# Second block of a two-block model kernel: banks of the attention gate, order and banks of the index products, bank of the key's rope, pace of attention

## The chip, the cores and the metric

The program runs on one core of a Trainium2 chip. The metric is the device time of one execution in microseconds, from the first to the last instruction with what lies around them. Engines are named as in the profile: PE is TensorE's matmuls, PEld its weight loads, DVE is VectorE, ACT is ScalarE, POOL is GpSimd, SP issues most DMAs.

## What is computed

The reference is a first block (gated delta rule, window attention, a feed-forward layer and a mixture of eight experts) followed by a second block of two layers. Only the second block is touched. Each of its layers does this on 256 rows of width 1024:

```python
h = rmsnorm(x, norm_g[l])
q, k, v, ga, iq, ik, iw, xr, gr, ma, mb = jnp.split(h @ w_in[l], offsets, axis=-1)
q, k = apply_rope(q), apply_rope(k)           # 8 heads of 128
iq, ik = apply_rope(iq), apply_rope(ik)       # 16 index heads of 64, one index key
...
dots = jnp.einsum('bqhd,bsd->bqhs', iqb, ik)
idx_score = jnp.einsum('bqh,bqhs->bqs', iwb, jax.nn.relu(dots))
_, sel = lax.top_k(idx_score, topk)           # 64 of up to 256 keys, per query
... # softmax attention of q over the chosen k, v
y_a = (attn * jax.nn.silu(ga)) @ w_out_attn[l]
hr = rg_lru(causal_depthwise_conv_2(xr, ...)) # gated linear recurrence
y_b = (hr * jax.nn.silu(gr)) @ w_out_rnn[l]
x = x + (sigmoid(ma) * y_a + sigmoid(mb) * y_b) @ w_o[l]
```

## The kernel before

**Weights.** All is float32. A projection is cut into tiles of 128 output columns. ScalarE casts the tile's weights to fp32r (`hi`, L1816), VectorE subtracts to get the low part (`lo`, L2436; "the split"), and TensorE does three fp32r matmuls for each of 8 slices of the depth (`mm3`, L864 to L866): 24 matmuls of 128x256 a tile. Five such weight slots exist in this part, so cast and split of a piece can run up to five tiles ahead. SP loads two tiles' weights with one DMA of 1 MB.

**Order of a layer.** Every engine has its own program in program order, tied by semaphores, and all of them walk through the same list (`fm(...)`, TensorE L1747 to L1772, ScalarE L2385 to L2406, VectorE L3272 to L3290): v, xr, ik and iw, iq, then q, k, ga (8 tiles each), gr (11), ma and mb (8 each), then the output products ya, yb and o. `fm` takes tiles in pairs; a pair fills one of the eight PSUM banks, and the banks in its third argument are used in turn. Before a bank is written, `claim(b)` waits for the step that was noted as its last reader. q and k use banks 0 to 3 and are emptied by ScalarE. ga and gr are emptied by ScalarE's tanh and then by VectorE, which multiplies by the bank once more (`silu`, L3258 to L3263).

**Side work in ticks.** Between tiles `fm` calls `tick()`, which runs one step of a generator. `ticks=2` gives one after each tile; `ticks=3` gives one after the first tile of a pair and two after the second. During q, k and ga the generator is `index_steps` (24 ticks, called I1 to I24 here); during gr and ma it is `attention_steps` (A1 on; gr gives 12 ticks, with A11 and A12 together after its eleventh tile). `also=rn` advances the recurrence (`rnn_steps`) by half a step after every second pair: its matmuls are L1739, on ScalarE it is tanh, exp and square root with table loads (L2364 to L2376), on VectorE four operations ending in a scan (L3244 to L3251), always some tiles behind ScalarE.

**Index.** I1 is the rope product of ik, I2 to I5 those of iq (`rope`, L1676): one matmul with a rotation matrix into bank 4 or 5, read by VectorE's first rope operation (L3154), after which two more follow (L3155, L3158). The bank is `4 + (i // 2) % 2`, so ik's and the first iq's are both in bank 4. From I7 on come the index products (L1701): 12 ticks, each filling one bank, 4 and 5 in turn, with products of 64 rows for two heads of 256 keys (eight ticks) or four heads of 128 keys (four ticks). A tick takes heads of one row half only: even heads lie in rows 0 to 63, odd ones in rows 64 to 127. ScalarE applies relu a bank per tick (L2343, two buffers), VectorE multiplies by iw and adds (L3190). After the last product VectorE picks the 64 greatest by eight rounds of max and match-replace (L3204, L3207).

**Attention.** A1 to A8 are the ropes of q and k in the same two banks, A9 is empty. Then six units of four 128x128 blocks go through `attend` (11 steps, A10 to A20): scores (L1713), mask and maximum on VectorE (L2783 to L2789), exponentials on ScalarE (L2110), reciprocal (L2797), scaling (L2126), transposes (L870, bank 4), their copy (L2118), products with v (L1721, bank 5), the gate (L3227).

Of the kernel before, what the change touches and what calls it, by code (L numbers as in the profile page):

```python
# [14 lines left out]
T = 256  # L15
# [14 lines left out]
C_ID, C_ONE, C_ROTA, C_ROTI, C_TRIL, C_LT, C_IOTA = range(7)  # L30
# [235 lines left out]
def _program(nc, ctx, p, out):  # L266
    S = Signals(nc, ctx)
    up, at = S.up, S.at
# [12 lines left out]
    bank = [ctx.enter_context(nc.psum_tensor(f"bank{i}", [128, 512], F32)) for i in range(8)]  # L281
# [24 lines left out]
    def C(k):  # L306
        return consts[:, k * 128:(k + 1) * 128]
# [546 lines left out]
    def tensor_program(pe):  # L854
# [4 lines left out]
        def claim(b):  # L859
            if b in busy:  # L860
                pe.wait_ge(*at(*busy[b]))
# [810 lines left out]
        for l in range(2):  # L1672
            t_ = T_l[l]
            if l == 0:
                h_cols(0, 0)
            def rope(Xt, n, rotc, name, l=l):  # L1676
                for i in range(0, n, 2):
                    m = min(2, n - i)
                    b = 4 + (i // 2) % 2
                    claim(b)  # L1680
                    pe.matmul(bank[b][:, 0:m * T], rotc, Xt[:, i:i + m, :].rearrange("p a b -> p (a b)"), start=True, stop=True).then_inc(*up("rot", l, name, i))
                    busy[b] = ("rot_sin", l, name, i)
                    yield

            def index_steps(l=l):
                pe.wait_ge(*at("iq", l, 6))
                yield from rope(L2.IK.unsqueeze(1), 1, C(C_ROTI), "ik")
                yield from rope(L2.IQ, 8, C(C_ROTI), "iq")
                yield
                pe.wait_ge(*at("roped", l, "iq", 6))  # L1690
                nr = 0
                for n in (1, 0):
                    wd = 128 * (n + 1)
                    nh = 512 // wd
                    for g in range(0, 16, 2 * nh):
                        for par in range(2):
                            b = 4 + nr % 2
                            claim(b)
                            for i in range(nh):
                                h = g + par + 2 * i  # L1700
                                k = pe.matmul(bank[b][:, i * wd:(i + 1) * wd], L2.IQ[64 * par:64 * par + 64, h // 2, n * 128:n * 128 + 128],  # L1701
                                              L2.IK[64 * par:64 * par + 64, 0:wd], start=True, stop=True)
                            k.then_inc(*up("dots", l, nr))
                            busy[b] = ("relu", l, nr)
                            nr += 1
                            yield
                for r in range(5):
                    yield

            def qk2(u, q, o, l=l):  # L1710
                hs, wd, n = u
                pe.wait_ge(*at("roped", l, "k", 6))
                return pe.matmul(o, L2.QT[:, hs[q], n * 128:n * 128 + 128], L2.KT[:, hs[q], 0:wd], start=True, stop=True)  # L1713

            def pv2(u, i, b, l=l):
                hs, wd, n = u
                nt = wd // 128
                pe.wait_ge(*at("v", l, 1, 1))
                for q in range(4):
                    h, kt = q // nt, q % nt  # L1720
                    k = pe.matmul(bank[b][:, h * 128:(h + 1) * 128], L2.VV[:, kt, hs[h] * 128:(hs[h] + 1) * 128], L2.pT[:, i % 2, q * 128:(q + 1) * 128], start=kt == 0, stop=kt == nt - 1)  # L1721
                return k

            def attention_steps(l=l):
                pe.wait_ge(*at("k", l, 6))
                yield from rope(L2.QT, 8, C(C_ROTA), "q")
                yield from rope(L2.KT, 8, C(C_ROTA), "k")
                yield
                yield from attend(DSA_UNITS, l, ((2, 3), (4,), (5,)), qk2, pv2, 2)

            def rnn_steps(l=l):

                for n in range(8):
                    h = 2 * (n % 2)
                    pe.wait_ge(*at("rnn_xc", l, n))
                    for q in range(2):
                        claim(6 + q)
                        for j in range(2):
                            k = pe.matmul(bank[6 + q][0:88, j * T:(j + 1) * T], L2.WR[:, q, h + j, :], L2.XC[:, h + j, :], start=True, stop=True)  # L1739
                    k.then_inc(*up("rnn_mm", l, n))  # L1740
                    busy[6], busy[7] = ("rnn_exp", l, n), ("rnn_ix", l, n)
                    yield
                    yield

            rn, ix, at_ = rnn_steps(), index_steps(), attention_steps()
            rm_first(t_["v0"][0], XT, (0, 1), (("h", l),), ("v", l, 0), lambda l=l: h_cols(l, 1))
            lane.back[:] = [rn]  # L1747
            fm(t_["xr"], XT, (2, 3, 0, 1), ("xr", l))
            rm(t_["v1"], XT, (0, 1), ("v", l), c0=1)
            tick()  # L1750
            x = t_["ik"]
            _, w = piece_view(W, x)
            pe.wait_ge(*at("lo", x))
            claim(4)
            for k in range(8):
                k_ = mm3(bank[4][:, 0:T], sl(w, ALL, k), sl(XT, ALL, k), k == 0, k == 7)
            k_.then_inc(*up("used", x))
            narrow(bank[4][:, T:T + 64], t_["iw"], 16, 4)
            busy[4] = ("iw", l)
            fm(t_["iq"], XT, (2, 3, 0, 1), ("iq", l), pace=lambda nb: nb % 2)  # L1760
            lane.back[:] = [ix]
            fm(t_["q"], XT, (0, 1, 2, 3), ("q", l), ticks=2, also=rn)
            fm(t_["k"], XT, (0, 1, 2, 3), ("k", l), ticks=2, also=rn)
            fm(t_["ga"], XT, (0, 1), ("ga", l), ticks=2, also=rn)
            lane.finish(ix)
            lane.back[:] = [at_]
            fm(t_["gr"], XT, (0, 1), ("gr", l), ticks=2, also=rn)
            fm(t_["ma"], XT, (0, 1), ("ma", l), ticks=3, also=rn)
            lane.finish(at_)
            lane.back[:] = [rn]  # L1770
            fm(t_["mb"], XT, (0, 1, 2, 3), ("mb", l), pace=lambda nb: 1)
            lane.finish(rn)  # L1772
            pe.wait_ge(*at("o_cols", l, 5))
            fm_raw(t_["ya"], L2.GA, (0, 1, 2, 3), ("ya", l), 8)
            pe.wait_ge(*at("hr_gated", l))
            fm_raw(t_["yb"], L2.GR, (0, 1, 2, 3), ("yb", l), 11)

            def o_ready(k, l=l):
                if k % 2 == 0:
                    pe.wait_ge(*at("lo_merge", l, k))  # L1780
            out_proj(XT, t_["o"], (4, 5, 6, 7), o_ready, (lambda: h_cols(1, 0)) if l == 0 else None)
            for t in range(2):
                for h in range(2):
                    busy[4 + 2 * t + h] = ("resid", l, t, h)
# [19 lines left out]
    def scalar_program(a):  # L1804
# [508 lines left out]
        for l in range(2):  # L2313
# [81 lines left out]
            lane.back[:] = [ix]  # L2395
            fm(t_["q"], to(L2.QT, "q"), ticks=2, also=rn)
            fm(t_["k"], to(L2.KT, "k"), ticks=2, also=rn)
            fm(t_["ga"], tanh_to(L2.GA, "ga_th", 2), ticks=2, also=rn)
            lane.finish(ix)
            lane.back[:] = [at_]  # L2400
            fm(t_["gr"], tanh_to(L2.GR, "gr_th", 2, [(f"xr_out{i}", l) for i in range(3)]), ticks=2, also=rn)
            fm(t_["ma"], tanh_to(L2.MA, "ma", 2), ticks=3, also=rn)
            lane.finish(at_)
            lane.back[:] = [rn]
            fm(t_["mb"], tanh_to(L2.MB, "mb", 4), pace=lambda nb: 1)
# [22 lines left out]
    def vector_program(v):  # L2428
# [714 lines left out]
        for l in range(2):  # L3143
            t_ = T_l[l]

            def rope(Xt, n, cos, sin, name, l=l, state=[None, None]):
                for i in range(0, n, 2):
                    m, s = min(2, n - i), (i // 2) % 2
                    x2 = Xt[:, i:i + m, :]
                    r_ = L2.rt[:, s, 0:m * T].rearrange("p (a b) -> p a b", a=m)  # L3150
                    v.wait_ge(*at("rot", l, name, i))
# [12 lines left out]

            def index_steps(l=l):
                v.wait_ge(*at("cos", 1))
                yield from rope(L2.IK.unsqueeze(1), 1, cosI, sinI, "ik")
                yield from rope(L2.IQ, 8, cosI, sinI, "iq")
                yield
                yield  # L3170
# [84 lines left out]
                    run(n)  # L3255
                    yield

            def silu(dst, name, l=l):  # L3258

                def f(i, m, nb, x):  # L3260
                    d = dst[:, i:i + m, :]
                    v.wait_ge(*at(name + "_th", l, i))
                    v.scalar_tensor_tensor(d, d, 1.0, bank[nb % 2][:, 0:m * T].rearrange("p (a b) -> p a b", a=m), ALU.add, ALU.mult).then_inc(*up(name, l, i))  # L3263
                return f

            def gated(l=l):
# [12 lines left out]
            lane.back[:] = [ix]  # L3279
            fm(t_["q"], None, ticks=2, also=rn)  # L3280
            fm(t_["k"], None, ticks=2, also=rn)
            fm(t_["ga"], silu(L2.GA, "ga"), ticks=2, also=rn)
            lane.finish(ix)
            lane.back[:] = [at_]
            fm(t_["gr"], silu(L2.GR, "gr"), ticks=2, also=rn)
            fm(t_["ma"], None, ticks=3, also=rn)
            lane.finish(at_)
            lane.back[:] = [rn]
            fm(t_["mb"], None, pace=lambda nb: 1)
# [137 lines left out]
```

## Time and profile before

| | us |
|---|---|
| median of 3 runs | 2372.04 |
| lowest, highest | 2367.88, 2376.61 |
| the profiled execution | 2379.05 |
| its span | 2377.2 |
| TensorE, VectorE, ScalarE busy | 2261.4, 1695.3, 1421.5 |

The second block's first layer begins at about 1550 us of the span, the second at about 1966 us. The profile gives the busy time of each engine, the granted clock of TensorE, groups of instructions by line, who waited for whom, and the instructions in order of time. A bracket behind an instruction, such as [2.87 <-DVE work L3154], is the idle time of its engine just before it and what ended that. Matmuls are pipelined: one may be shown to start before the last has ended. A float32 matmul that is not fp32r shows as two records.

### The profile page before, as it was taken

How to read it: one execution, taken by the hardware profiler on the slowest of the kernel's cores; microseconds unless marked ns; L12 is line 12 of the kernel's file. 1: busy time of each engine (PE TensorE's matmuls, PEld its weight loads, DVE VectorE, ACT ScalarE, POOL GpSimd, SP SyncE). 2: the span in 40 equal slices, each digit the busy share in tenths (PEclk: the TensorE clock that was granted, in tenths of full speed). 3: DMA queues.
4: the chain of work that ended last, by engine and by line, in shares of the span. 5: the costliest groups of instructions: out<-in, count | busy, mean ns of one | idle time of the engine just before them, and what ended most of it. 6: DMA issues, size and time to landing. Idle time of an engine off the chain costs nothing.

```text
span 2377.2 us, 34395 instructions
## 1 busy us (share of the span) xinstructions
PE 2261.4 (95%) x13903; PEld 1984.1 (83%) x13903; DVE 1695.3 (71%) x2152; ACT 1421.5 (60%) x1894; POOL 316.0 (13%) x314
## 2 busy tenths in 40 slices
PE   7889999989999999999999999979998999999898
PEld 7778999877878888888888888769887988888897
DVE  5634655778899999999899999754687335469624
ACT  5432444556787878787777778645556324555722
POOL 0510000000000000000000000006445002553400
PEclk9899999998999999999999999989999999999999
DMA  9421655528899999999999999837444465644343
GB/s 249 126 80 64 233 193 173 173 72 292 315 371 376 363 350 367 356 361 349 363 355 356 357 354 367 305 103 226 131 124 133 125 220 162 193 140 129 114 134 109
DMA packets 328397, 556.42 MB, mean 234 GB/s; under 512 B 23616, under 2 KB 164680, under 8 KB 328232
## 3 DMA queue, kind: packets, MB, share of 16 engines
q1 hardware_dynamic: 318432, 527.63, 63.7%
q0 software_dynamic: 9120, 25.97, 4.6%
q8 instruction: 113, 1.85, 0.3%
q10 hardware_dynamic: 680, 0.54, 0.1%
q14 instruction: 52, 0.43, 0.1%
HBM read 544.12 MB, written 9.96 MB: 233 GB/s over the span
## 4 chain that ended last, share of the span: by engine, by line
PE 82%; DVE 12%; ACT 4%; issue 2%; DMA 0%; SPq 0%; ACTq 0%; DVEq 0%
PE bank L864 22%; PE bank L866 22%; PE bank L865 22%; PE bank L905 6%; DVE parts L2436 3%; PE bank L870 1%; ACT parts L1816 1%; PE bank L1533 1%; PE bank L1701 1%; PE bank L1739 1%; DVE fast L2436 1%; PE bank L1019 1%; PE bank L1594 1%; DVE work L3154 1%; DVE work L3155 1%
## 5 line engine op out<-in xcount | busy, mean ns | idle before, releaser
L2436 DVE TENSOR_TENSOR parts<-raw,parts 128x1024 fp32r<-128x1024 f32 x665 | 809.2, 1231 | 400.7 <-ACT parts L1816 377.3
L1816 ACT CAST parts<-raw 128x1024 fp32r<-128x1024 f32 x665 | 692.0, 1047 | 504.3 <-PE bank L866 490.6
L864 PE MATMUL bank<-cols,parts 128*128 128x256 f32 x1680 | 501.0, 298 | 14.8 <-DVE parts L2436 5.7
L866 PE MATMUL bank<-cols,parts 128*128 128x256 f32 x1680 | 481.9, 287 | 1.1 <-issue 1.1
L865 PE MATMUL bank<-cols,parts 128*128 128x256 f32 x1680 | 482.2, 287 | 0.0
L2436 DVE TENSOR_TENSOR fast<-raw,fast 128x1024 fp32r<-128x1024 f32 x302 | 362.1, 1219 | 32.1 <-ACT fast L1816 14.9
L1816 ACT CAST fast<-raw 128x1024 fp32r<-128x1024 f32 x302 | 315.7, 1052 | 94.1 <-PE bank L866 87.3
L864 PEld LDWEIGHTS bank<-cols,parts 128*128 128x128 f32 x1680 | 330.1, 196 | 32.6 <-issue 19.8
L865 PEld LDWEIGHTS bank<-cols,parts 128*128 128x128 f32 x1680 | 330.1, 196 | 6.2 <-issue 5.4
L866 PEld LDWEIGHTS bank<-cols,parts 128*128 128x128 f32 x1680 | 329.2, 196 | 0.0
L864 PE MATMUL bank<-parts,cols 128*128 128x512 f32 x740 | 294.2, 398 | 13.6 <-DVE parts L2436 6.9
L866 PE MATMUL bank<-parts,cols 128*128 128x512 f32 x740 | 290.6, 393 | 0.0
L865 PE MATMUL bank<-parts,cols 128*128 128x512 f32 x740 | 290.4, 392 | 0.0
L864 PEld LDWEIGHTS bank<-parts,cols 128*128 128x128 f32 x740 | 140.1, 189 | 44.7 <-DVE parts L2436 7.8
L866 PEld LDWEIGHTS bank<-parts,cols 128*128 128x128 f32 x740 | 140.3, 190 | 29.8
L865 PEld LDWEIGHTS bank<-parts,cols 128*128 128x128 f32 x740 | 140.3, 190 | 28.1
L864 PE MATMUL bank<-fast,cols 128*128 128x512 f32 x380 | 149.0, 392 | 0.8 <-DVE fast L2436 0.8
L866 PE MATMUL bank<-fast,cols 128*128 128x512 f32 x380 | 147.9, 389 | 0.0
L865 PE MATMUL bank<-fast,cols 128*128 128x512 f32 x380 | 147.9, 389 | 0.0
L797 POOL DMA_DIRECT2D scr_xr<-work x6 | 4.9, 809 | 1027.0 <-ACT work L2319 1027.0
L905 PE MATMUL bank<-work,raw 128*128 128x256 f32 x608 | 132.1, 378 | 0.0
L905 PEld LDWEIGHTS bank<-work,raw 128*128 128x128 f32 x608 | 114.8, 189 | 16.7
(376 smaller groups left out, 3278.1 us busy)
## 6 DMA issues: line engine op xcount, KB each, us to landing
raw<-in_moe_w_gate_dram SPq DMA_DIRECT2D x112, 1024.0 KB, 6.1
raw<-in_moe_w_up_dram SPq DMA_DIRECT2D x112, 1024.0 KB, 5.9
raw<-in_moe_w_down_dram SPq DMA_DIRECT2D x112, 1024.0 KB, 6.1
raw<-in_w_in_dram SPq DMA_DIRECT2D x76, 1024.0 KB, 5.5
raw<-in_a_w_in_dram SPq DMA_DIRECT2D x12, 1024.0 KB, 11.7
raw<-in_ffn_w_gate_dram SPq DMA_DIRECT2D x11, 1024.0 KB, 5.2
raw<-in_ffn_w_up_dram SPq DMA_DIRECT2D x11, 1024.0 KB, 5.2
raw<-in_ffn_w_down_dram SPq DMA_DIRECT2D x11, 1024.0 KB, 5.0
```

What stands on the lines that cost most here:

```text
L864: pe.matmul(o, l[0], r[0], start=start, stop=False)
L865: pe.matmul(o, l[0], r[1], start=False, stop=False)
L866: return pe.matmul(o, l[1], r[0], start=False, stop=stop)
L870: return pe.transpose(o, i, ident[0:n, 0:n])
L905: k_ = pe.matmul(bank[b][:, j * T:(j + 1) * T], w[:, k, q * 128:(q + 1) * 128], xt[:, k, :], start=k == 0, stop=k == kt - 1)
L1019: k = pe.matmul(o[rs, 64 * j:64 * j + 64], l[rs, j, :], r[rs, j, :], start=True, stop=True)
L1533: k = pe.matmul(bank[b][:, j * 128:(j + 1) * 128], X[:, t, kk * 128:(kk + 1) * 128], N4.P_[:, a, t, :], start=t == 0, stop=t == 1)
L1594: k = pe.matmul(bank[b][:, :], N4.PT[:, e % 2, t, :], N4.y[:, q, 512 * h:512 * h + 512], start=q == 0, stop=q == 1)
L1701: k = pe.matmul(bank[b][:, i * wd:(i + 1) * wd], L2.IQ[64 * par:64 * par + 64, h // 2, n * 128:n * 128 + 128], L2.IK[64 * par:64 * par + 6 ...
L1739: k = pe.matmul(bank[6 + q][0:88, j * T:(j + 1) * T], L2.WR[:, q, h + j, :], L2.XC[:, h + j, :], start=True, stop=True)
L1816: a.copy(dst[0], src).then_inc(*up(o + "hi", x))
L2436: v.tensor_tensor(dst[1], src, dst[0].bitcast(F32), ALU.subtract).then_inc(*up(o + "lo", x))
```

## The change

Four edits, all in the second block and the same in both layers:

- ik's rope product and its VectorE buffer use the other of the two banks (5 instead of 4), with the index `odd=1`.
- An index tick claims banks 4 and 5 together and issues the products of both row halves in alternation, an even head into bank 4 and then an odd one into bank 5; the next tick issues none. ScalarE and VectorE keep a bank per tick.
- ga uses banks 0 to 3 in place of 0 and 1, on all three engines.
- ma's `ticks` is 2 in place of 3.

TensorE's part, then ScalarE's and VectorE's lines:

```diff
-            def rope(Xt, n, rotc, name, l=l):
+            def rope(Xt, n, rotc, name, odd=0, l=l):
                 for i in range(0, n, 2):
                     m = min(2, n - i)
-                    b = 4 + (i // 2) % 2
+                    b = 4 + (i // 2 + odd) % 2
                     claim(b)
...
-                yield from rope(L2.IK.unsqueeze(1), 1, C(C_ROTI), "ik")
+                yield from rope(L2.IK.unsqueeze(1), 1, C(C_ROTI), "ik", 1)
...
                     for g in range(0, 16, 2 * nh):
-                        for par in range(2):
-                            b = 4 + nr % 2
-                            claim(b)
-                            for i in range(nh):
-                                h = g + par + 2 * i
-                                k = pe.matmul(bank[b][:, i * wd:(i + 1) * wd], L2.IQ[64 * par:64 * par + 64, h // 2, n * 128:n * 128 + 128],
-                                              L2.IK[64 * par:64 * par + 64, 0:wd], start=True, stop=True)
-                            k.then_inc(*up("dots", l, nr))
-                            busy[b] = ("relu", l, nr)
-                            nr += 1
-                            yield
+
+                        claim(4)
+                        claim(5)
+                        for i in range(nh):
+                            for par in range(2):
+                                rs, h = slice(64 * par, 64 * par + 64), g + par + 2 * i
+                                k = pe.matmul(bank[4 + par][:, i * wd:(i + 1) * wd], L2.IQ[rs, h // 2, n * 128:n * 128 + 128], L2.IK[rs, 0:wd], start=True, stop=True)
+                                if i == nh - 1:
+                                    k.then_inc(*up("dots", l, nr + par))
+                                    busy[4 + par] = ("relu", l, nr + par)
+                        nr += 2
+                        yield
+                        yield
...
-            fm(t_["ga"], XT, (0, 1), ("ga", l), ticks=2, also=rn)
+            fm(t_["ga"], XT, (0, 1, 2, 3), ("ga", l), ticks=2, also=rn)
...
-            fm(t_["ma"], XT, (0, 1), ("ma", l), ticks=3, also=rn)
+            fm(t_["ma"], XT, (0, 1), ("ma", l), ticks=2, also=rn)
...
-            fm(t_["ga"], tanh_to(L2.GA, "ga_th", 2), ticks=2, also=rn)
+            fm(t_["ga"], tanh_to(L2.GA, "ga_th", 4), ticks=2, also=rn)
...
-            fm(t_["ma"], tanh_to(L2.MA, "ma", 2), ticks=3, also=rn)
+            fm(t_["ma"], tanh_to(L2.MA, "ma", 2), ticks=2, also=rn)
...
-                    m, s = min(2, n - i), (i // 2) % 2
+                    m, s = min(2, n - i), (i // 2 + odd) % 2
...
-            fm(t_["ga"], silu(L2.GA, "ga"), ticks=2, also=rn)
+            fm(t_["ga"], silu(L2.GA, "ga", 4), ticks=2, also=rn)
...
-            fm(t_["ma"], None, ticks=3, also=rn)
+            fm(t_["ma"], None, ticks=2, also=rn)
```

## Rows read from the trace of the kernel before

**Rows 1.** The page, busy time of the engines over the span:
```profile
PE 2261.4 (95%) x13903; PEld 1984.1 (83%) x13903; DVE 1695.3 (71%) x2152; ACT 1421.5 (60%) x1894; POOL 316.0 (13%) x314
```

**Rows 2.** Windows: stretch, length, busy PE, PEld, DVE, ACT, POOL, clock, DMA, GB/s:
```profile
1670.25:1673.40 3.15, 3.15 (x9) 2.12 (x9) 2.88 (x5) 0.00 (x0) 0.05 (x1) 0.50 0.85 246
1690.00:1740.00 50.00, 49.61 (x342) 43.75 (x343) 28.13 (x39) 33.20 (x50) 29.43 (x27) 1.00 0.46 142
1740.00:1757.70 17.70, 17.70 (x148) 17.58 (x147) 16.98 (x42) 9.01 (x11) 0.74 (x1) 1.00 0.31 91
...
1762.36:1765.70 3.34, 3.34 (x16) 3.34 (x17) 3.24 (x13) 2.57 (x4) 3.16 (x4) 0.50 0.04 15
1765.70:1790.00 24.30, 24.12 (x166) 20.52 (x165) 23.85 (x45) 9.16 (x10) 6.12 (x7) 1.00 0.46 143
...
1822.50:1825.50 3.00, 2.94 (x16) 2.80 (x17) 2.66 (x5) 2.38 (x8) 2.82 (x4) 0.72 0.46 161
```

**Rows 3.** Waits of TensorE, 1655 to 1880: total us, times, longest:
```profile
PE bank L870 <- ACT work L2118: 5.8, 2, 4.1
PE bank L1681 <- DVE work L3154: 4.3, 2, 2.9
PE bank L864 <- DVE work L3263: 2.7, 1, 2.7
PE bank L1721 <- issue: 0.9, 1, 0.9
PE bank L1713 <- DVE work L3158: 0.8, 1, 0.8
PE bank L1701 <- DVE work L3158: 0.5, 1, 0.5
```

**Rows 4.** Timeline of TensorE: start, length, line; rope products I2 to I4, gr:
```profile
1670.25 1.22 PE L1681 MATMUL bank<-work 128*128 128x512 f32 x1 [2.87 <-DVE work L3154]
...
1675.67 1.02 PE L1681 MATMUL bank<-work 128*128 128x512 f32 x2
...
1679.39 1.02 PE L1681 MATMUL bank<-work 128*128 128x512 f32 x2
...
1762.36 0.52 PE L864 MATMUL bank<-cols,parts 128*128 128x256 f32 x1 [2.74 <-DVE work L3263]
```

**Rows 5.** Timeline of TensorE, two of the index products' ticks:
```profile
1700.34 1.13 PE L1701 MATMUL bank<-work 64*128 64x256 f32 x4
...
1704.46 1.13 PE L1701 MATMUL bank<-work 64*128 64x256 f32 x4
```

**Rows 6.** Timeline of TensorE, first block: window scores, row halves in alternation:
```profile
475.52 1.23 PE L1463 MATMUL bank<-work 64*128 64x256 f32 x8
```

**Rows 7.** Timeline of VectorE: splits, iq's rope, recurrence, q's first rope:
```profile
1668.63 1.23 DVE L2436 TENSOR_TENSOR parts<-raw,parts 128x1024 fp32r<-128x1024 f32 x1 [6.54 <-ACT parts L1816]
...
1672.36 0.69 DVE L3154 TENSOR_TENSOR work<-bank,work 128x512 f32<-128x512 f32 x1 [0.24 <-PE bank L1681]
...
1683.74 0.68 DVE L3244 SCALAR_TENSOR_TENSOR work<-bank,work 88x512 f32<-88x512 f32 x1
...
1686.97 1.20 DVE L2436 TENSOR_TENSOR parts<-raw,parts 128x1024 fp32r<-128x1024 f32 x1
...
1738.98 1.23 DVE L2436 TENSOR_TENSOR parts<-raw,parts 128x1024 fp32r<-128x1024 f32 x1 [4.83 <-ACT parts L1816]
...
1774.10 0.68 DVE L3154 TENSOR_TENSOR work<-bank,work 128x512 f32<-128x512 f32 x1
```

**Rows 8.** Timeline of ScalarE: relu, transposes' copy, recurrence's first and last operation:
```profile
1714.25 0.60 ACT L2343 ACTIVATE work<-bank 128x512 f32<-128x512 f32 x1
...
1821.85 0.57 ACT L2118 COPY work<-bank 128x512 f32<-128x512 f32 x1
...
1839.88 1.52 ACT L2364 ACTIVATE bank<-bank,work 88x256 f32<-88x256 f32 x4 [2.04 <-PE bank L1739]
...
1844.56 0.63 ACT L2376 ACTIVATE work<-work 88x512 f32<-88x512 f32 x1
```

More of the change, by code:

```diff
@@ L3144, in vector_program, with rope @@
             t_ = T_l[l]
-            def rope(Xt, n, cos, sin, name, l=l, state=[None, None]):
+            def rope(Xt, n, cos, sin, name, odd=0, l=l, state=[None, None]):
                 for i in range(0, n, 2):
-                    m, s = min(2, n - i), (i // 2) % 2
+                    m, s = min(2, n - i), (i // 2 + odd) % 2
                     x2 = Xt[:, i:i + m, :]
@@ L3166, in index_steps @@
                 v.wait_ge(*at("cos", 1))
-                yield from rope(L2.IK.unsqueeze(1), 1, cosI, sinI, "ik")
+                yield from rope(L2.IK.unsqueeze(1), 1, cosI, sinI, "ik", 1)
                 yield from rope(L2.IQ, 8, cosI, sinI, "iq")
@@ L3256, in rnn_steps, with silu @@
                     yield
-            def silu(dst, name, l=l):
+            def silu(dst, name, banks, l=l):
                 def f(i, m, nb, x):
@@ L3262, in f @@
                     v.wait_ge(*at(name + "_th", l, i))
-                    v.scalar_tensor_tensor(d, d, 1.0, bank[nb % 2][:, 0:m * T].rearrange("p (a b) -> p a b", a=m), ALU.add, ALU.mult).then_inc(*up(name, l, i))
+                    v.scalar_tensor_tensor(d, d, 1.0, bank[nb % banks][:, 0:m * T].rearrange("p (a b) -> p a b", a=m), ALU.add, ALU.mult).then_inc(*up(name, l, i))
                 return f
@@ L3281, in vector_program @@
             fm(t_["k"], None, ticks=2, also=rn)
-            fm(t_["ga"], silu(L2.GA, "ga"), ticks=2, also=rn)
+            fm(t_["ga"], silu(L2.GA, "ga", 4), ticks=2, also=rn)
             lane.finish(ix)
             lane.back[:] = [at_]
-            fm(t_["gr"], silu(L2.GR, "gr"), ticks=2, also=rn)
-            fm(t_["ma"], None, ticks=3, also=rn)
+            fm(t_["gr"], silu(L2.GR, "gr", 2), ticks=2, also=rn)
+            fm(t_["ma"], None, ticks=2, also=rn)
             lane.finish(at_)
```

## Prediction

> **What bounds the kernel now.** I read the page first: TensorE (PE) is busy 2261.4 of 2377.2 us, so what is left is small waits, and matmul time that an edit removes [rows 1]. The edits lie in the second block only, in a part that runs once in each of its two layers, 1663 to 1879 us in the first one. Next came TensorE's waits there: six kinds, 15.0 us in all, and in the second layer the same list with the same figures [rows 3]. So I work out one layer and double it. The two long waits that end at 1670.25 and 1762.36 us are each followed by some 3 us at a granted clock of 0.50, that is 1.2 GHz in place of 2.4; the 4.1 us wait is followed by 3 us at 0.72 [rows 2]. A wait thus costs more than itself: from the rope product at 1670.25 to the next is 5.42 us, from that to the one after 3.72 [rows 4], so the low clock cost 1.7 us.
>
> Then the windows by stage. From 1690 to 1740 us (index products) VectorE is busy 28.1 of 50 us, and TensorE is the bound. From 1740 to 1790 us and beyond VectorE is full: 16.98 of 17.70, 23.85 of 24.30 us [rows 2]. It has its last real idle stretch, 4.83 us, at 1738.98 [rows 7], and from there to the last attention scores every TensorE wait is a wait for something VectorE makes. **This second stretch, over 80 us, is as long as VectorE's work in it.** What TensorE saves before it counts only as far as VectorE's stretch starts earlier; what it saves inside counts nothing. Behind it TensorE is the bound again, through the last gate and the output products. Ticks are numbered I1 to I24 for the index (q, k, ga tiles) and A1 on for attention (gr, ma tiles). A tile of 24 matmuls takes 2.87 us: 148 matmuls fill 17.70 us [rows 2].
>
> **Key's rope in bank 5.** Now the first iq rope (I2) claims the bank of ik's rope and waits 2.87 us until VectorE has read it; VectorE itself was held by the weight split at 1668.63 [rows 4, 7]. In its own bank this wait goes, with its 1.7 us of low clock, and the first index product would lose its 0.5 us wait: 5.1 us. But four ropes and one recurrence step must pass VectorE before I7. VectorE was idle for 0.24 us before its first iq rope at 1672.36, so it is free for it at 1672.1; then come four ropes of three operations, some 1.95 us each (0.69 us an operation), three splits of 1.14 and the recurrence, 1683.74 to 1686.97, 3.2 us [rows 7]: 7.8+3.4+3.2 = 14.4, ending at 1686.5. TensorE reaches I7 now at 1679.39 (I4) + 3.72 + 0.85 + 2x2.87 = 1689.7 [rows 4], and 4.57 us earlier at 1685.1. A new wait of 1.4 us stands at I7; I take the clock to hold, since the waits that it fell after are of 2.7 us or more [rows 2, 3]. Gain: 5.1 - 1.4 = **3.7 us**. Bounds: 5.1, and 0 if ScalarE's earlier casts were late as well.
>
> **Index products in pairs.** Twelve ticks carry one bank of products each. The period is 4.12 us [rows 5], less 2.87: 1.25 us a bank. No row shows index products of alternating row halves. The nearest are the first block's window scores, whose 64-row products are issued in just that order into two banks: eight records take 1.23 us, against 1.13 for four of one half [rows 5, 6]. I take that 0.10 more: 1.35 for a pair in place of 2.50. The bounds are no saving (halves one after another) and half, 1.25. The Trainium skill, page "TensorEngine Tiling (Array Packing)", section "Key Properties", says that changing the tiling mode drains TensorE; entering the half-array mode six times and not twelve would by that rule save edges too, and the sum has it in the one 1.25 taken per pair. The same page, section "PSUM Bottleneck", speaks against the change: tiling speeds TensorE up but not the emptying of PSUM. Here ScalarE empties the banks, busy 33.2 of 50 us, and that would still fit in 45 [rows 2].
>
> The new wait: a pair claims both banks, so it needs the relu of the second half, which ScalarE does one tick later, behind a cast and at times a copy. Behind this claim on TensorE stand all its tiles. A relu now ends at 1714.85, 2.15 us after its tile (1704.46 + 2x4.12) [rows 5, 8]; the next pair comes 2.87 after: 0.7 us to spare. After I8 ScalarE also has a recurrence step, 5.3 us and a table load of 1.28 [rows 8]; I follow it through: cast, relu, cast, copy, relu end 12.2 us after I8's tile, TensorE claims at 11.6. One wait of 0.6. To I16 nine singles (11.25) become five pairs (6.75): 4.5 - 0.6 = **3.9 us**. The saving after I16, 2.4 us, falls into VectorE's stretch. VectorE resumes at 1738.98 after a ScalarE cast that hangs on I16's tile [rows 7]; so its stretch starts 3.7 + 3.9 = **7.6 us** earlier, its order and work unchanged.
>
> **Four banks for the attention gate.** Now gr's first tile waits 2.7 us for VectorE's SiLU of the third ga pair [rows 3]. With four banks this wait goes. What is late next: the third q rope (A3) claims bank 4, which VectorE frees at 1774.78, when the first operation of its first q rope ends [rows 7]. TensorE would be there at 1762.36 - 2.74 (wait) - 10.0 (gain up to I18) + 3 tiles (8.6) + 2 ropes (1.7) = 1760, the release comes at 1774.78 - 7.6 = 1767.2. So one wait of 7 us takes the place of 2.7 and two small ones, and 1.7 us of low clock follow, as before. VectorE is not held up (it has the next two ropes' products ahead), so I cost the edit at **nothing**; its cover is VectorE's own queue, and if that should run dry the low clock costs 1.7 a layer.
>
> **Attention over all of the gate ma.** Three ticks per pair of tiles become two, 20 steps in 20 ticks. No DMA is moved, and SP's and POOL's queues keep their order; VectorE and ScalarE do the same steps, each one tile later. Steps A14, A15 now stand back to back, and A15's transposes wait 4.1 us for ScalarE's copy of the first ones, ending 1822.42 [rows 3, 8]. With a tile between, 2.9 of the 4.1 are used. A17, A18 (1.7 us wait) and the last products (0.9) get tiles between too [rows 3]: 2.6. The idle shortened at A15 spares about 0.8 us of clock at 0.72 [rows 2]. Against that, the recurrence step of ScalarE (5.3 us, [rows 8]) now falls after A16, ahead of the copy that A18 needs. Followed through: the step cannot start before A16's casts, scaling, copy and exponentials end, 4.3 us after A16; plus 5.2, cast 0.9, scaling 0.8, copy 0.6 is 11.8; TensorE is at A18 after 9.8 (1.25+1.55+2.9+1.25+2.9). A new wait of 2.0. No later one: A19 comes 4.1 after A18, when ScalarE has just finished. Net: 2.9+2.6+0.8-2.0 = 4.3; around each wait that goes the trace also has edges of 0.1 to 0.2 us (the list of waits leaves them out), some 0.7 in all by my estimate. I take **5.0 us**. Bounds: 2.9 (all else handed back) and 7.
>
> **Sum.** 7.6 + 0 + 5.0 = 12.6 us a layer, 25.2 in two. The profiled execution took 2379.05 us, 7.0 above the median of the runs, and gives 2353.9; against the median, 2372.0 - 25.2 = **2346.8 us**.
>
> **Rivals.** (a) The halves do not overlap, or only as far as VectorE cannot use it: 3.7 + 5.0 = 8.7 a layer, 2354.6 us. For: index operands lie differently from the window's. Against: [rows 6]. (b) VectorE's stretch is not rigid: waits inside it shrink as casts come earlier, the new A18 wait stays out; 16 a layer, 2340 us. The outer bound, all waits (15), low clock (3.8) and pair savings (6.9), is 26 a layer, 2320. (c) VectorE starts no earlier, because ScalarE, not TensorE, sets its cast at 1738.98: then only the attention part is left, 10 us in two layers, 2362 us; the change hardly does what it says. (d) **Slower**: the claim of both banks. If the second relu comes a whole tile late, each of five pair claims waits 2.9 us and 1.7 of low clock follow, 23 us a layer, against gains of 6.9+3.7+5.0 = 15.6: 7.4 lost a layer, 2387 us. It decides the sign when ScalarE lags its tile by 4.3 us rather than 2.15 at each pair (a wait of 1.4 and 1.7 of clock, 3.1 each). For it: one claim is already short. Against: ScalarE is busy only two thirds here [rows 2]. The Trainium skill, page "TensorE: Matmul & The Clock Gate", section on the HAM clock gate, states that an idle TensorE falls back to 1.2 GHz; the 0.50 after 2.87 us agrees [rows 2, 3]. A3's wait of 7 us is where it would strike anew.
>
> **From cases to numbers.** Forecast 0.50, (a) 0.15, (b) 0.14, (c) 0.14, (d) 0.07. The range reaches to (a) and (b) with their bounds, 2337 to 2360, and leaves (c) and (d) out. A measurement of this kernel tells about 0.5% (12 us) from no change: faster 0.79 (forecast, a, b), same 0.14 (c), slower 0.07 (d).
>
> **What would show it.** Right: no wait at I2, a short one at I7; twelve half-array bursts per layer become six of 1.2 to 1.3 us; gr's first tile without a wait and a wait of about 7 us ahead of A3, followed by clock 0.50; VectorE idle last some 7.6 us earlier, counted from the layer's ik rope; about 1 us ahead of A15, 2 at A18. Wrong: bursts of 2.2 us (a), VectorE's stretch shortened (b) or unmoved (c), a wait for relu at every pair (d). All is off if weights come late: the faster tiles need casts and chunks sooner.

## Result and profile after

The changed kernel takes 2348.07 us in the median of 4 runs (2340.6 to 2350.82), the kernel before 2371.29 (4 runs). The ratio is 0.9895, 95% interval 0.9866 to 0.9925; in a later comparison of the same two kernels it was 0.9877 (0.9862 to 0.9892, 2344.16 us in the median of 5 runs). The profiled execution took 2350.82 us with a span of 2349.0, 28.2 us less than the profiled one before. Its engines, from the page; VectorE's and ScalarE's work is the same, TensorE's busy time is 24 us less [rows 1]:

```profile
PE 2237.4 (95%) x13903; PEld 1967.3 (84%) x13903; DVE 1695.4 (72%) x2152; ACT 1420.0 (60%) x1894; POOL 318.9 (14%) x314
```

**Length of a layer.** To compare kernels I take the time from the ik rope product (I1) to the first product with ya's raw weights (L905), since the start of the second block varies from run to run (the ik rope comes at 1664.88 us in one run of the changed kernel and at 1656.60 in another) and hides what a layer gains. Before, TensorE's timeline:

```profile
1663.92 0.60 PE L1681 MATMUL bank<-work 128*128 128x256 f32 x2
...
1879.30 0.81 PE L905 MATMUL bank<-work,raw 128*128 128x256 f32 x3
```

and after:

```profile
1664.88 0.60 PE L1681 MATMUL bank<-work 128*128 128x256 f32 x2
...
1866.57 0.60 PE L905 MATMUL bank<-work,raw 128*128 128x256 f32 x2
```

So 215.38 us before (216.09 in the second layer) and 201.69 after (202.21; 201.66 and 201.70 in the later run): 13.7 us less in the first layer, 13.9 in the second. The two together are the 28.2 us between the profiled executions to within 1 us. The medians are only 23.2 us apart, which is within the scatter of single executions (10 us for the changed kernel). Line numbers behind L1700 are one or two higher than before.

**Waits of TensorE** in the first layer, 1655 to 1870 us, as in [rows 3]:

```profile
PE bank L1681 <- DVE work L3156: 7.2, 1, 7.2
PE bank L870 <- ACT work L2120: 2.2, 2, 1.2
PE bank L1702 <- DVE work L3160: 1.6, 1, 1.6
PE bank L1702 <- ACT work L2345: 1.0, 1, 1.0
PE bank L1715 <- DVE work L3160: 0.8, 1, 0.8
```

12.8 us in place of 15.0 [rows 3]: waits explain 2.2 us of the 13.7. The rest is matmul time: six bursts of products in place of twelve (some 7.5 us) and one stretch of low clock in place of three (some 3 us by my estimate, from the stretches below); about 1 us is left to small gaps. The timeline shows where the new waits are, at I7, I11, A3, A15 and A18, and between them a burst of products that no wait precedes (1711.55) and the rope product that follows A3's (1773.71). Some rows hold fewer records than the burst has, because the stretch that was read ends inside it:

```profile
1687.70 0.49 PE L1702 MATMUL bank<-work 64*128 64x256 f32 x2 [1.58 <-DVE work L3160]
...
1704.55 0.70 PE L1702 MATMUL bank<-work 64*128 64x256 f32 x4 [1.02 <-ACT work L2345]
...
1711.55 1.13 PE L1702 MATMUL bank<-work 64*128 64x256 f32 x8
...
1768.12 1.22 PE L1681 MATMUL bank<-work 128*128 128x512 f32 x1 [7.21 <-DVE work L3156]
...
1773.71 0.59 PE L1681 MATMUL bank<-work 128*128 128x512 f32 x1
...
1815.83 0.63 PE L870 MATMUL bank<-work 128*128 128x128 f32 x4 [1.24 <-ACT work L2120]
...
1832.49 0.52 PE L870 MATMUL bank<-work 128*128 128x128 f32 x3 [0.93 <-ACT work L2120]
```

**Windows** of the same layer (columns as in [rows 2]): index products; VectorE's full stretch up to A3; the 3.3 us after the long wait; from there to the attention scores (A10); the 3 us after A15:

```profile
1688.00:1740.00 52.00, 50.98 (x416) 47.65 (x413) 33.56 (x51) 37.46 (x55) 29.37 (x27) 1.00 0.49 152
1733.00:1768.10 35.10, 27.90 (x217) 26.28 (x215) 34.05 (x91) 21.10 (x28) 14.52 (x15) 0.96 0.40 122
1768.12:1771.40 3.28, 3.28 (x9) 2.25 (x10) 3.25 (x5) 0.00 (x0) 0.00 (x0) 0.50 0.89 272
1771.40:1798.00 26.60, 25.88 (x181) 22.69 (x179) 26.29 (x36) 13.13 (x20) 14.19 (x11) 0.99 0.49 148
...
1815.83:1818.80 2.97, 2.97 (x23) 2.86 (x24) 2.55 (x5) 2.97 (x8) 2.80 (x3) 1.00 0.35 122
```

After the wait of 7.21 us the clock is at 0.50 for 3.28 us, and the low clock costs 1.9 us; after the one of 2.87 us it was 3.15 us and 1.7 us [rows 2, 4]. So here the one long wait costs about as much low clock as one short one did. After A15 the clock is 1.00 in place of 0.72. That 0.72 is a mean over a stretch that begins before the clock falls; in the kernel before, TensorE was at 0.50 here as well, only from some 1.3 us behind the end of the wait:

```profile
1824.00:1827.00 3.00, 3.00 (x16) 3.00 (x15) 2.26 (x5) 2.37 (x7) 2.92 (x3) 0.50 0.01 3
```

VectorE's last idle stretch before it is full ends 67.59 us after the ik rope, and not at 75.06 as before [rows 7], so its stretch starts 7.5 us earlier:

```profile
1732.47 1.22 DVE L2438 TENSOR_TENSOR parts<-raw,parts 128x1024 fp32r<-128x1024 f32 x1 [4.66 <-ACT parts L1818]
```

From there to the first attention scores (A10) it does the same work in the same time, 65.72 us before (first row, from the old trace) and 65.53 after:

```profile
1738.98:1804.70 65.72, 60.62 (x427) 54.22 (x426) 64.20 (x130) 35.00 (x49) 28.66 (x26) 0.97 0.45 136
...
1732.47:1798.00 65.53, 57.60 (x409) 51.76 (x407) 64.14 (x130) 34.76 (x49) 28.71 (x26) 0.95 0.46 141
```

### The profile page after: what moved, and what is told of

The parts are those of the page before. It is cut to its first block, busy times and chain, and to the rows that moved or that the text cites. A ratio compares the mean times of both kernels' runs of the same rounds, so it can differ in the third digit from the quotient of the medians.

```text
span 2349.0 us, 34405 instructions
## 1 busy us (share of the span) xinstructions
PE 2237.4 (95%) x13903; PEld 1967.3 (84%) x13903; DVE 1695.4 (72%) x2152; ACT 1420.0 (60%) x1894; POOL 318.9 (14%) x314
## 4 chain that ended last, share of the span: by engine, by line
PE 79%; DVE 12%; ACT 6%; issue 2%; POOL 1%; DMA 0%; SPq 0%; ACTq 0%; DVEq 0%; POOLq 0%
PE bank L864 22%; PE bank L866 21%; PE bank L865 21%; PE bank L905 6%; DVE parts L2438 3%; ACT parts L1818 2%; PE bank L870 1%; PE bank L1533 1%; PE bank L1019 1%; DVE fast L2438 1%; ACT work L2375 1%; PE bank L1594 1%; POOL work L728 1%; DVE work L3209 1%; ACT bank L2366 1%
## 5 line engine op out<-in xcount | busy, mean ns | idle before, releaser
L905 PE MATMUL bank<-work,raw 128*128 128x256 f32 x608 | 132.1, 378 | 0.0
L905 PEld LDWEIGHTS bank<-work,raw 128*128 128x128 f32 x608 | 114.8, 189 | 16.7
```

Source lines behind the costliest of these rows:

```text
L905: k_ = pe.matmul(bank[b][:, j * T:(j + 1) * T], w[:, k, q * 128:(q + 1) * 128], xt[:, k, :], start=k == 0, stop=k == kt - 1)
```

## Experiments

Theory: up to some point VectorE's work sets the time, and what TensorE saves ahead of it counts only as far as that stretch starts earlier. Rival: each edit is worth the TensorE time that it removes. The first four kernels each undo one edit of the change; "layer" is the length defined above, first and second layer. Where no number of runs is given, the kernel was run once. Since the executions of one kernel scatter over some 10 us, such a run is read by its layers, which for the changed kernel were 201.69 and 202.21 in one run and 201.66 and 201.70 in another: differences of 0.5 us are within the scatter.

**Key's rope back in bank 4.**

```diff
-                yield from rope(L2.IK.unsqueeze(1), 1, C(C_ROTI), "ik", 1)
+                yield from rope(L2.IK.unsqueeze(1), 1, C(C_ROTI), "ik")
```

(and VectorE's line likewise)

> The change with one edit undone: the key's rope is in bank 4 again. Measured length: from the ik rope product to the first product with the raw weights (ya), per layer; 215.4 us before, 201.7 us with the change. Theory (the stretch in which VectorE is full starts later by what TensorE loses ahead of it): the 2.9 us wait at I2 and 1.7 us of low clock are back, the 1.6 us wait at I7 mostly goes, so the layer is longer by 3.7 us: 205.4, the whole kernel by 7.4. Rival (each edit is worth the TensorE time that it removes by itself): 2.9 + 1.7 + 0.5, 206.8. Rival 2 (the gain is swallowed ahead of VectorE's stretch): 201.7.

Measured: 2356.17 us, layer 205.36 and 206.38. The first layer is the theory's 205.4 and not the rival's 206.8. In the second VectorE's full stretch begins 1.3 us later than in the first (72.3 and 71.0 us after the ik rope); why is not shown. The wait of 2.86 us at I2 is back, that at I7 is 0.5 again.

**Index products in twelve ticks again** (TensorE's loop as in the kernel before).

> The change with the index products undone: twelve ticks of one bank again. Theory (VectorE's stretch): what twelve bursts of 1.25 us cost more than six of 1.26 counts up to tick I16 only, less the 1.0 us wait at I11: 4 x 1.25 - 0.05 - 1.0 = 3.9, layer 205.6, and TensorE's wait ahead of A3 shrinks from 7.2 us by the 2.4 us that TensorE loses after I16. Rival (TensorE's own time counts everywhere): 6 x 1.25 - 1.0 = 6.4, layer 208.1, wait ahead of A3 unchanged.

Measured: 2353.8 us, layer 205.70 and 205.93: the theory's 205.6, 2.4 us below the rival. TensorE's waits show that the part of the saving behind I16 had only been waited away again; its wait ahead of A3 is 4.9 in place of 7.2:

```profile
PE bank L1681 <- DVE work L3155: 4.9, 1, 4.9
PE bank L870 <- ACT work L2119: 2.1, 2, 1.2
PE bank L1702 <- DVE work L3159: 1.6, 1, 1.6
PE bank L1714 <- DVE work L3159: 0.8, 1, 0.8
```

**Attention gate back on two banks.**

```diff
-            fm(t_["ga"], XT, (0, 1, 2, 3), ("ga", l), ticks=2, also=rn)
+            fm(t_["ga"], XT, (0, 1), ("ga", l), ticks=2, also=rn)
```

(and the bank counts on ScalarE and VectorE)

> The change with the attention gate back on two banks. Theory (VectorE's stretch): nothing, layer 201.7 within 0.5 us: a wait of some 5 us for the SiLU stands at gr's first tile and the one ahead of A3 shrinks to 1 us or less; VectorE's first q rope starts as long after the ik rope as with the change (102.5 us). Rival (the four banks bring what the removed wait and its low clock cost): longer by 2.7 + 1.5 = 4 us, 206.

Measured: 2350.07 us, layer 201.60 and 201.59. The four banks bring nothing. TensorE now waits 5.0 us for the SiLU at gr's first tile and 1.0 at A7 for a rope, in place of 7.2 ahead of A3, and VectorE's first q rope starts at the same time, 102.4 us after the ik rope (102.5 with the change):

```profile
PE bank L864 <- DVE work L3265: 5.0, 1, 5.0
PE bank L870 <- ACT work L2120: 2.2, 2, 1.2
PE bank L1702 <- DVE work L3160: 1.6, 1, 1.6
PE bank L1702 <- ACT work L2345: 1.0, 1, 1.0
PE bank L1681 <- DVE work L3156: 1.0, 1, 1.0
PE bank L1715 <- DVE work L3160: 0.8, 1, 0.8
```

**Three ticks per pair for ma again.**

```diff
-            fm(t_["ma"], XT, (0, 1), ("ma", l), ticks=2, also=rn)
+            fm(t_["ma"], XT, (0, 1), ("ma", l), ticks=3, also=rn)
```

> The change with three ticks per pair for the gate ma again. Nothing ahead of A14 moves. Waits of 4.1 us at A15, 1.7 at A18 and 0.9 at the end return, those of 1.2 and 0.9 go, the low clock after A15 returns. Theory: the layer is longer by 6.0 us, what the stretch from A15 to ya shortened by: 207.7. Rival (the gain behind A15 came from the earlier start of ScalarE's and VectorE's steps, not from the spacing): 203 or less.

Measured: 2357.6 us, layer 207.80 and 207.97: 6.1 us longer in the first layer, all behind A14. The waits of 4.11, 1.66 and 0.90 us are back. Together the four edits undone one by one cost 3.7 + 4.0 - 0.1 + 6.1 = 13.7 us in the first layer, which is the whole gain of that layer: there they don't interact. In the second layer they cost 4.2, 3.7, -0.6 and 5.8 us, 13.0 before rounding, of 13.9; the scatter of the layers can explain that gap.

**Both banks claimed, but one half after the other.**

```diff
-                        for i in range(nh):
-                            for par in range(2):
+                        for par in range(2):
+                            for i in range(nh):
```

> The change with both banks claimed at once as in it, but the products of the even heads all issued before those of the odd heads. Theory (matmuls of different row halves overlap only when they alternate): a burst takes 2.2 to 2.4 us in place of 1.13 to 1.16, VectorE's full stretch starts 5 x 1.1 less the wait at I11, some 4.5 us later, layer 206. Rival (a burst is short because the matmuls of one tick pay one change of array mode): 1.2 us and 201.7.

Measured: 2344.39 us, layer 202.39 and 202.17, which neither expected. The bursts of eight records are as short as with alternation; those of sixteen are longer, 1.71 us against 1.16. TensorE's timeline of this kernel:

```profile
1705.98 1.14 PE L1702 MATMUL bank<-work 64*128 64x256 f32 x8
...
1713.00 1.71 PE L1702 MATMUL bank<-work 64*128 64x128 f32 x16
```

and of the changed kernel:

```profile
1718.57 1.16 PE L1702 MATMUL bank<-work 64*128 64x128 f32 x16
```

So the halves do overlap, since 1.14 us is what four records of one half take alone [rows 5], but alternation is not needed for it when a half has four records. With eight it matters: the burst is 0.55 us longer, though still shorter than two bursts of one half. One such burst lies ahead of I16, and the product at A3 comes 0.5 us later after the ik rope (103.75 in place of 103.24 us); the layers themselves, 0.7 us longer and not longer at all, are too close to the scatter to show it. What in the array or its queue allows the overlap, these runs don't tell.

**More TensorE work in VectorE's stretch.** The product of A1 is issued four times more, into the same bank with the same operands:

```diff
+                    for _ in range(4 if (name, i) == ("q", 0) else 0):
+                        pe.matmul(bank[b][:, 0:m * T], rotc, Xt[:, i:i + m, :].rearrange("p a b -> p (a b)"), start=True, stop=True)
```

> The change with the first q rope product (A1) issued five times over, the same matmul into the same bank: 4 x 0.85 = 3.4 us more of TensorE work inside the stretch in which VectorE is full. Theory: the wait ahead of A3 shrinks from 7.2 to 3.8 us and the layer stays at 201.7. Rival (TensorE is the bound throughout): 205.1.

Measured: 2345.47 us, layer 202.18 and 201.66. The 3.4 us vanish in the wait, which is 3.76 us now:

```profile
PE bank L1683 <- DVE work L3158: 3.8, 1, 3.8
...
```

**More VectorE work behind A3.** The first operation of the first k rope is done three times more:

```diff
+                    for _ in range(3 if (name, i) == ("k", 0) else 0):
+                        v.tensor_tensor(r_, bank[4 + s][:, 0:m * T]..., sin..., ALU.mult).then_inc(*up("dve"))
+                        v.wait_ge(*at("dve"))
```

> The change with the first operation of the first k rope (A5) done four times over on VectorE: 3 x 0.65 = 1.9 us more of VectorE work inside its full stretch. Theory: the layer is longer by 1.9 us, 203.6, and the wait ahead of A3, which lies before, keeps 7.2. Rival (VectorE has slack there, TensorE is the bound): 201.7.

Measured: 2348.76 us, layer 204.27 and 204.57, 2.6 and 2.4 us longer for the 2.1 us that the three operations take. VectorE has no slack there; whether TensorE has, this run doesn't ask. The three waits for it under one heading, 9.7 us in all, are the old 7.2 and two new ones, 1.9 and 0.6:

```profile
PE bank L1681 <- DVE work L3159: 9.7, 3, 7.2
...
```

**Less VectorE work behind A3.** q's ropes move to the index ticks in which TensorE has no products; for that k's tiles use banks 0 and 1 only and the ropes banks 2 and 3. TensorE's part:

```diff
+                early = rope(L2.QT, 8, C(C_ROTA), "q", 0, 2)
...
                         nr += 2
                         yield
+                        if nr == 4:
+                            pe.wait_ge(*at("q", l, 6))
+                        if nr >= 4:
+                            next(early, None)
                         yield
...
-                yield from rope(L2.QT, 8, C(C_ROTA), "q")
+                for _ in range(4):
+                    yield
```

> The change with q's four ropes taken out of VectorE's full stretch: they run in the product-free ticks I10, I12, I14 and I16 (banks 2 and 3; k's tiles use banks 0 and 1), and A1 to A4 are empty. VectorE is idle for 17.7 us between I7 and I18 with the change. Theory: VectorE's stretch loses 4 x 1.95 = 7.8 us of work, of which up to 2 may come back where ropes delay the weighting and so the relus ahead of I11 to I16; layer 194 to 196, kernel some 12 to 15 us faster than with the change. Rival (another engine, ScalarE with its casts or the A15 chain, is next within 2 us): layer 200 or more.

Measured: 2345.12 us (4 runs), 0.9883 of the kernel before (0.9866 to 0.9899), layer 202.34 and 201.24: nothing over the change. Here the theory fell, and only the rival's number stood. 7.8 us of VectorE work are gone from behind A3, and the waits say what came in their place:

```profile
PE bank L864 <- DVE work L3275: 4.8, 1, 4.8
PE bank L870 <- ACT work L2126: 2.3, 2, 1.3
PE bank L864 <- DVE parts L2444: 2.1, 1, 2.1
PE bank L1703 <- DVE work L3166: 1.6, 1, 1.6
...
```

TensorE waits at gr's fourth tile for a split and at its fifth for gr's first SiLU on bank 0. Both stand in VectorE's queue among or behind the rounds that pick the 64 greatest. From there to A15 it has no wait at all, and now it is TensorE that is full, VectorE no longer:

```profile
1771.40:1811.00 39.60, 38.90 (x275) 35.29 (x274) 35.12 (x50) 24.57 (x53) 22.22 (x20) 0.96 0.52 156
```

In VectorE's timeline of the changed kernel the last operation of the top-k (L3219) ends at 1766.3 us, one split follows, and then the first rope operation, whose end lets TensorE go at 1768.12:

```profile
1766.03 0.30 DVE L3219 TENSOR_SCALAR work<-work 128x256 f32<-128x256 f32 x1
1766.24 1.22 DVE L2438 TENSOR_TENSOR parts<-raw,parts 128x1024 fp32r<-128x1024 f32 x1
1767.38 0.68 DVE L3156 TENSOR_TENSOR work<-bank,work 128x512 f32<-128x512 f32 x1
```

So the wait ahead of A3 is one for **the end of the top-k**, and behind it TensorE, let go late and at half clock, is about as full as VectorE (25.88 and 26.29 of 26.60 us with the change, in the windows above). Slowing VectorE there costs time, and relieving it alone brings nothing. That slowing TensorE there would cost as well is likely but was not tried: the extra work at A1 lay ahead of the wait.

**The same, and gr on four banks**, so that no gr tile needs a SiLU from behind the top-k:

```diff
-            fm(t_["gr"], XT, (0, 1), ("gr", l), ticks=2, also=rn)
+            fm(t_["gr"], XT, (0, 1, 2, 3), ("gr", l), ticks=2, also=rn)
```

> The version with q's ropes early, and gr's tiles on banks 0 to 3 in place of 0 and 1. In the version without this edit TensorE had no wait ahead of A3 any more but one of 2.1 us for a split and one of 4.8 us for gr's first SiLU on bank 0, each followed by low clock, and none from there to A15: layer 202.3 and 201.2 us. Theory (the wait ahead of A3 is a wait for the end of VectorE's top-k, and after it TensorE is the bound as much as VectorE): the 4.8 us and its 1.7 us of low clock go, VectorE's last k rope, which ends some 7 us ahead of A10 + 6.5, is next at A10 with a wait of 4 to 5 us; layer 199 to 200. Rival (VectorE's total work to the attention scores sets the end, whatever the bank): 201 to 202.

Measured: 2332.25 us in its one run, layer 197.53 and 197.57, 4.1 us below the change. The wait of 4.8 us and its low clock went; 1.8 to 2.3 us at A7 and 0.8 at A10, both for k's ropes, came back. That is below the theory's 199 to 200, and not the rival's. One reason is in the trace of the run before: behind its wait of 4.8 us the clock stayed at 0.50 for 5.3 us, 1768.15 to 1773.40, where the theory priced a low clock of 1.7 us. The change with gr on four banks alone, without the early ropes, was not run; since the changed kernel has no wait at any gr tile, I expect nothing of it, but that is argued and not shown.

**k's ropes in A1 to A4 on top of it.**

```diff
-                for _ in range(4):
-                    yield
                 yield from rope(L2.KT, 8, C(C_ROTA), "k")
-                yield
+                for _ in range(5):
+                    yield
```

> As the one before, with k's four ropes in A1 to A4 and the empty ticks in A5 to A8. Theory: the wait at A10 goes too, because the last k rope is done some four ticks earlier; of waits only some 2 us for a split before the end of the top-k, one at A15 and one at A18 stay; layer 195 to 197, kernel 10 to 14 us faster than with the change. Rival (splits behind the ropes become late, TensorE waits for weights in gr): 200 or more.

Measured: 2348.47 us (5 runs), 0.9895 (0.9881 to 0.9908), layer 202.39 and 202.28: the whole gain is lost. I had overlooked that A3's rope then claims bank 4 again before VectorE, still in its top-k, has read A1's. The timeline of TensorE has a wait of 8.29 us there:

```profile
1772.21 2.08 PE L1681 MATMUL bank<-work 128*128 128x512 f32 x2 [8.29 <-DVE work L3161]
```

VectorE's top-k ends at 1770.4 us in this run. As an experiment it confirms what the wait is for: any rope product at A3 that follows one at A1 is held until the top-k ends, q's or k's.

**The changed kernel again, and the best version timed.** Each of these two was compared with the kernel before on its own chip, so they are compared with each other by their ratios.

> The changed kernel once more, beside the other versions and the kernel before on the same chip. Every theory: 0.99 of the kernel before, layer 201.7 to 202.2.

Measured: 2344.16 us (5 runs), ratio 0.9877 (0.9862 to 0.9892), layer 201.66 and 201.70.

> The version with q's ropes early and gr on four banks, timed. Its single run took 2332.25 us and its layers 197.5 us, 4.15 less than with the change. From the layers: 2 x (215.7 - 197.5) = 36.4 us under the kernel before, ratio 0.985 (0.983 to 0.987). If the single run's 41 us stood, 0.983; if the shorter layers were lost elsewhere, 0.988 as with the change.

Measured: 2337.72 us (5 runs, 2332.01 to 2338.51), ratio 0.9841 (0.9827 to 0.9854), layer 197.54 twice. It beats both kernels: 1.6% under the kernel before, and its interval does not meet that of the change. Its waits in the first layer:

```profile
PE bank L864 <- DVE parts L2444: 2.9, 2, 2.1
PE bank L1681 <- DVE work L3162: 2.3, 1, 2.3
PE bank L870 <- ACT work L2126: 2.2, 2, 1.2
PE bank L1703 <- DVE work L3166: 1.6, 1, 1.6
PE bank L1720 <- DVE work L3166: 0.8, 1, 0.8
PE bank L1703 <- ACT work L2351: 0.2, 1, 0.2
```

## The prediction, step by step

Forecast 2346.8 us, measured 2348.07; forecast 12.6 us a layer, measured 13.7 and 13.9. That the total is met within 1.3 us is partly luck: the layers gained 2.4 us more than forecast in all, while the median of the first comparison shows 4.4 us less than the layers do. The later comparison, 2344.16 us, fits the layers better.

**Key's rope, 3.7 us: right.** I7 comes 3.65 us earlier after the ik rope than before, the new wait there is 1.58 us where 1.4 was forecast, and undoing the edit costs 3.7.

**Index products, 3.9 us up to I16: right in sum, with two terms off that cancel.** A pair costs no more than a single bank: 1.13 us for eight records, as long as four took [rows 5], where the window scores let me add 0.10 [rows 6]. The wait at I11 is 1.0 and not 0.6. Undoing the edit costs 4.0. That the claim of both banks would wait for the relu one tick later showed at I11 alone; the slower rival (d), which needed this at every pair, is out. Its break-even also priced 1.7 us of low clock behind waits of 1.4 us; behind the measured ones of 1.58 and 1.02 us the clock stayed at 1.00. ScalarE, which empties the banks, was busy 37.5 of 52 us in the products' stretch. The Trainium skill, page "TensorEngine Tiling (Array Packing)", section "PSUM Bottleneck", says that tiling speeds up TensorE but not the emptying of PSUM; here that shows as the one wait at I11 and not as a bound.

**Four banks for the gate, nothing: right.** The wait ahead of A3 was forecast at 7.2 us (1767.2 less 1760) and is 7.21, with 1.9 us of low clock (5.59 us to the next rope product, against 3.72 in [rows 4]). Undoing the edit costs -0.1.

**Attention over all of ma, 5.0 us: mis-sized, 6.1 measured.** The mechanism is as described: the wait at A15 shrank from 4.11 to 1.24 (forecast some 1.2), A17 and the last products wait no more, and the recurrence step makes a new wait at A18. The term that was off is that wait, 2.0 forecast and 0.93 measured. TensorE came to A18 10.6 us after A16 and not 9.8, ScalarE's copy ended 11.4 after it and not 11.8. This one term is the 1.1 us between forecast and result, if the other two are taken together: the low clock spared behind A15 was put at 0.8 us, from the mean of 0.72, and is some 1.5 by my estimate, 3 us at 0.50; that leaves nothing for the 0.7 us of "edges", which no row shows by themselves. Their sum, 1.5, was right by a high guess beside a low one. (The table load of 1.28 us is in ScalarE's timeline, but not among the lines of [rows 8].)

**"It is as long as VectorE's work in it": half right.** For the part up to the end of the top-k it holds: 34.05 of 35.10 us busy, and 3.4 us more TensorE work are free. For the part behind A3 the step failed: I read full VectorE windows as the bound, but TensorE there is full too (25.88 of 26.60 us), and taking 7.8 us of work from VectorE brought nothing. The sum did not suffer, because both parts start earlier by the same amount. Rivals (a), (b) and (c) are out as well: the halves overlap, and VectorE's stretch moved by 7.5 us with its work and, within 0.2 us, its length unchanged.

## What to carry to other kernels

Where two engines take turns as the bound, price an edit by how much earlier it lets the next full stretch start, and follow each removed wait to the next claim that will stop the engine: here a wait of 2.7 us came back as one of 7.2, for a later step of the same VectorE queue. A window in which one engine is full does not prove it the bound; look whether the other one waits in it. If a wait stays although more banks were given to the work it was put down to, ask which single step in the other engine's queue all the releases are behind, and move work from behind it together with the banks that let the waiting engine pass.

## What the runs showed of the hardware

Products of 64 rows for both row halves took as long as those for one half: 1.13 us for eight records as for four, 1.16 for sixteen as for eight. The starts agree: two tiles and a burst of eight records take 1.28 us more than the two tiles alone (1711.55 to 1718.57 us, less 2 x 2.87), one with four took 1.25 more. With four records a half, it made no difference whether the halves alternate; with eight a half, one after the other cost 0.55 us more (1.71 us). And the clock was at 0.50 for some 3.3 us after a wait of 7.2 us, as it was after waits of 2.7 and 2.9 us, but for 5.3 us after the one of 4.8 us in the run with early q ropes. The length of a wait alone does not tell whether the clock falls: behind a wait of 2.1 us for the same split it fell to 0.50 within 1.5 us in the first run of the version with gr on four banks, and it stayed at 1.00 in the timed one.
